# Gate halves stored in eight pieces, one per tile, and four down tiles that take the last gates from SBUF

## What is computed

```python
idx = e1 * N_KEYS + e2                       # N_KEYS = 128, so 128 x 128 experts
gates = jax.nn.softmax(sc, axis=-1)
u = peer_u[ix]
a = jax.nn.gelu(jnp.einsum('td,thkd->thk', hx, u), approximate=False)
vsel = peer_v[ix]
return jnp.einsum('thk,thkd->td', gx * a, vsel)
```

## Time and profile before

| | |
|---|---|
| median of 3 runs | 3111.55 us (3110.08 to 3111.72) |
| the profiled execution | 3113.11 us, span 3111.4 us |
| TensorE busy | 2941.4 us (95%) |
| VectorE, ScalarE, GpSimd busy | 1801.4, 1118.9, 1814.2 us |
| bytes moved | 539.11 MB, mean 173 GB/s |
| stores of gates | 12 of 2048 KB, median 16.3 us to landing |
| up stage | about 375 to 1090 us |
| down stage | about 1092 to 1600 us |

### The profile page before, as it was taken

The page is one execution under the profiler, slowest core; times in us unless marked ns, Lnnn a source line. Parts: engine busy times, 40 slices in busy tenths (PEclk is TensorE's granted clock), DMA queues, the critical chain, the costliest instruction groups (busy, mean ns, idle before and its releaser), DMA issues. The chain is left out here.

```text
span 3111.4 us, 42451 instructions
## 1 busy us (share of the span) xinstructions
PE 2941.4 (95%) x14433; PEld 2468.3 (79%) x14433; DVE 1801.4 (58%) x2994; ACT 1118.9 (36%) x2318; POOL 1814.2 (58%) x1154
## 2 busy tenths in 40 slices
PE   6989999998898889999999989999999999999998
PEld 5757899997898878888887667888778887788886
DVE  7764269977654377888874443322377887423225
ACT  2232215554455235444443423220145552322103
POOL 5525686676787745555543234666657664466664
PEclk9999999999999999999999999999999999999999
DMA  8412254566688989999972012223221111222332
GB/s 312 149 70 83 96 162 142 184 220 237 223 298 290 334 338 400 407 406 396 409 281 75 28 55 82 100 94 102 94 82 64 59 61 48 81 94 94 102 102 74
DMA packets 167757, 539.11 MB, mean 173 GB/s; under 512 B 15584, under 2 KB 73056, under 8 KB 151136
## 3 DMA queue, kind: packets, MB, share of 16 engines
q1 hardware_dynamic: 82544, 301.62, 27.9%
q0 software_dynamic: 18432, 134.23, 10.9%
q10 hardware_dynamic: 66672, 101.99, 9.0%
HBM read 485.35 MB, written 52.43 MB: 173 GB/s over the span
## 5 line engine op out<-in xcount | busy, mean ns | idle before, releaser
L2527 POOL TENSOR_SCALAR whi<-ring 128x1024 fp32r<-128x1024 f32 x384 | 426.0, 1109 | 989.6 <-issue 514.1
L2529 POOL TENSOR_TENSOR wlo<-ring,whi 128x1024 fp32r<-128x1024 f32 x384 | 972.1, 2532 | 32.1
L561 PE MATMUL ps<-norm_hi,whi 128*128 128x384 f32 (+1 forms) x1288 | 494.0, 384 | 20.6 <-ACT A L1413 11.9
L563 PE MATMUL ps<-norm_hi,wlo 128*128 128x384 f32 (+1 forms) x1288 | 454.5, 353 | 0.0
L562 PE MATMUL ps<-norm_lo,whi 128*128 128x384 f32 (+1 forms) x1288 | 453.1, 352 | 0.0
L561 PE MATMUL ps<-whi,mixed_hi 128*128 128x512 f32 x768 | 300.5, 391 | 11.5 <-DVE wlo L2123 8.7
L562 PE MATMUL ps<-wlo,mixed_hi 128*128 128x512 f32 x768 | 299.6, 390 | 0.0
L563 PE MATMUL ps<-whi,mixed_lo 128*128 128x512 f32 x768 | 299.5, 390 | 0.0
L2553 POOL TENSOR_TENSOR wlo<-ring,whi 128x512 fp32r<-128x512 f32 x126 | 166.2, 1319 | 228.5 <-ACT whi L1517 228.5
L561 PE MATMUL ps<-mix_hi,whi 128*128 128x512 f32 x744 | 290.6, 391 | 0.0
L563 PE MATMUL ps<-mix_hi,wlo 128*128 128x512 f32 x744 | 289.5, 389 | 0.0
(11 more groups left out here) (362 smaller groups left out, 6013.4 us busy)
## 6 DMA issues: line engine op xcount, KB each, us to landing
ring<-stream SPq DMA_DIRECT2D x519, 512.0 KB, 3.4
gelu_map<-A ACTq DMA_DIRECT2D x128, 192.0 KB, 2.9
gate_map<-A ACTq DMA_DIRECT2D x12, 2048.0 KB, 16.3
A<-gelu_map ACTq DMA_DIRECT2D x128, 192.0 KB, 10.8
A<-gate_map ACTq DMA_DIRECT2D x32, 768.0 KB, 13.0
A<-ada_w SPq DMA_DIRECT2D x10, 2048.0 KB, 8.1
A<-ada_w SPq DMA_DIRECT2D x4, 1024.0 KB, 22.7
X<-x_in SPq DMA_DIRECT2D x1, 2048.0 KB, 18.9
```

Source lines behind the costliest of these rows:

```text
L561: first = mm(out_, lh, rh, start=start, stop=False)
L563: return first, mm(out_, ll, rh, start=False, stop=stop)
L2527: g.tensor_scalar(h[:], raw[:], 1.0, 0.0, ALU.mult, ALU.add).then_inc(whi_ready, 1)
L2529: g.tensor_tensor(rest[:], raw[:], h[:].bitcast(F32), ALU.subtract).then_inc(split_ready, 1)
```

## The change

- A half is stored in eight pieces of 512 KB, one DMA each, instead of two of 2048 KB. A piece goes out at the end of ScalarE's work for each of the first eight tiles (b % 16 < 8) of the next half. The last half goes out in two pieces in each of the first four tail tiles.
- The counts: one semaphore for the first halves (eight pieces, 128 a phase), two for the second halves (four pieces, 64 a phase each). All waits on stores follow.
- In the tail, the eight loads of Gelu rows go out two a tile in tiles 0 to 3. The first load of gates goes out at k = 2 and takes five of six parts; the last 64 tokens' gates of the first four down tiles come from `staging[1]`, with a second, small product of VectorE. The load for the tiles from 4 on stays at k = 5.
- The high and low parts of the mixed rows change places (planes 36 to 39 and 32 to 35), and the first low part waits until all four mixes have read the staging plane.

```diff
+PIECES = 8
-PARTS_AT = dict(mixed=(32, 36), ...
+PARTS_AT = dict(mixed=(36, 32), ...
-            def store_gates(phase, half):
+            def store_gates(phase, half, e):
                 act.wait_ge(gate_bank_free, 2 + phase * AMONG + (half + 1) * AMONG // 2)
-                for q in range(2):
-                    g = slice(q * NKEY // 8, (q + 1) * NKEY // 8)
-                    r = slice(q * NKEY // 2, (q + 1) * NKEY // 2)
-                    act.dma_start(gate_map[g, :, 2 * phase + half, :].rearrange("g j n -> j g n"),
-                                  staging[half][:, r, :].rearrange("p (g i) t -> p g (i t)", i=4)).then_inc(gate_stored[q], 16)
+                g = slice(e * NKEY // 4 // PIECES, (e + 1) * NKEY // 4 // PIECES)
+                r = slice(e * NKEY // PIECES, (e + 1) * NKEY // PIECES)
+                act.dma_start(gate_map[g, :, 2 * phase + half, :].rearrange("g j n -> j g n"),
+                              staging[half][:, r, :].rearrange("p (g i) t -> p g (i t)", i=4)).then_inc(gate_stored[half and 1 + e // 4], 16)
                     if phase and b % 16 == 0:
-                        for q in range(2):
-                            act.wait_ge(gate_stored[q], 16 * (2 * phase - 1 + half))
+                        for part in ((0,), (1, 2))[half]:
+                            act.wait_ge(gate_stored[part], (128, 64)[half] * phase)
-                    if b % 16 == 15:
-                        store_gates(phase, half)
+                    if b % 16 < PIECES and (phase or half):
+                        store_gates(phase - 1 + half, 1 - half, b % 16)
-            def load_gates(m):
+            def load_gates(m, parts=2 * len(DENSE)):
-                act.dma_start(gate_ring[:, m // 4 % 2], gate_map[m // 4:m // 4 + 1].rearrange("g j b n -> (g j) b n"))\
+                act.dma_start(gate_ring[:, m // 4 % 2, 0:parts, :],
+                              gate_map[m // 4:m // 4 + 1, :, 0:parts, :].rearrange("g j b n -> (g j) b n"))\
-                if k == 1 or k == 3:
-                    for q in range(2):
-                        act.wait_ge(gate_stored[q], 16 * 5)
-                    for s in range(4):
-                        load_mixed(2 * (k - 1) + s)
+                if k < 4:
+                    for e in range(2 * k, 2 * k + 2):
+                        store_gates(len(DENSE) - 1, 1, e)
+                    act.wait_ge(gate_stored[0], 128 * len(DENSE))
+                    for s in range(2 * k, 2 * k + 2):
+                        load_mixed(s)
+                if k == 2:
+                    load_gates(0, 2 * len(DENSE) - 1)
                 if k == 5:
-                    for q in range(2):
-                        act.wait_ge(gate_stored[q], 16 * 6)
-                    for m in (0, 4):
-                        load_gates(m)
+                    for part in (1, 2):
+                        act.wait_ge(gate_stored[part], 64 * len(DENSE))
+                    load_gates(4)
+                if n >= 4:
+                    v.tensor_tensor(a, a, gate, ALU.mult).then_inc(mixed_ready, 1)
+                    return
+                dve.wait_ge(gate_bank_free, 2 + len(DENSE) * AMONG)
+                last = 2 * len(DENSE) - 1
+                v.tensor_tensor(a[:, 0:last, :], a[:, 0:last, :], gate[:, 0:last, :], ALU.mult)
+                v.tensor_tensor(a[:, last, :], a[:, last, :], staging[1][:, n, :], ALU.mult).then_inc(mixed_ready, 1)
+                if n == 0:
+                    dve.wait_ge(mixed_ready, 4)
             for n in range(4):
                 mix(n)
-                if n:
-                    low_mixed(n - 1)
+            for n in range(3):
+                low_mixed(n)
```

## The result

| | before | after |
|---|---|---|
| median | 3111.64 us (3110.08 to 3114.05, 4 runs) | 3088.03 us (3085.86 to 3088.54, 4 runs) |
| profiled execution, span | 3113.11, 3111.4 us | 3088.54, 3086.8 us |
| ratio of the times | | 0.9913, 95% interval 0.9899 to 0.9927 |

The change takes 23.6 us off by the medians, 24.6 us by the two profiled spans; the step sum had 26.5. The sum is close, but two of its terms were wrong in opposite directions. Where the time came from is read in three places. In all rows that follow, three points stand for rows left out.

The account below looks back on a forecast made before the run. TensorE, 95% busy, was taken to bound the kernel, stalled through ScalarE's held store issues. 28 us mid-phase plus 3 tail less 4.5 pressure gave 26.5 off 3113.11, so 3086.6, or 3085.0 at the median; range 3069 to 3103.

Parts of the forecast that it names:

- pairs 1 and 2: Gate stores at about 552 and 635 us: no long TensorE stall, 0 to 1 us lost, 0.5 us given back.
- pair 3: Gate stores at about 740 us: 12.9 us lost over four tiles, 9 given back (bounds 5 and 12.9).
- pair 4: Gate stores at about 847 us: 7.0 us lost over two plain and two one-hot tiles, 6.5 given back.
- pair 5: Gate stores at about 948 us: 13.3 us lost over four tiles, 12 given back.
- pressure of pieces in phase 2: Pieces in 16 tiles of phase 2 fill the DMA engines, up to 12 gathers late; 4.5 us lost (bounds 0 and 10).
- tail stretch: Last Gelu copies to first down product, DMA engines full: 3 us gained, bounds 0 and 13.
- Rival 2: Issues of pieces still block ScalarE, the tail loses 5 and late gathers cost 10: 13 us gained, 3098.5; chance 0.20.
- VectorE is next late: At the third pair, VectorE's own work nearly fills four tiles of 5.1 us, so only 9 of 12.9 us return.
- Rival 4: VectorE is late on its own at the third to fifth pairs; within 6 us of before; chance 0.05.
- the sum that begins with "17.5 MB": Tail: 17.5 MB less 1.2 already moved, at 0.392 MB per us, takes 41.6 us; first down product at 1091.7.
- Rival 1: TensorE rules the tail and phase 2 absorbs the pieces: 40 us gained, 3071.5; chance 0.18.
- The rule on batches: Skill advice to batch transfers to 1 MiB and more; a 512 KB piece costs up to 0.1 us more, 5 us DMA time.

Follow-up runs that it names:

- repeat: The changed kernel run and profiled once more with nothing changed; 3089.5 us, ratio 0.9922 to the kernel before.
- the tail in order of need: Changed kernel with tail Gelu stores on SyncE, first four mixed-row loads and first gates load ahead of the pieces, fifth mix behind first down tile; 3085.62 us, ratio 0.9912.

## Why the prediction was right, and where it was not

Forecast 3085.0 (3069 to 3103), measured 3088.03. By its own terms (spans; 24.6 us in all):

| term | forecast | measured |
|---|---|---|
| pairs 1 and 2, up to tile 69 | +0.5 | -2.4 |
| pair 3 (69-85) | +9 | +8.8 |
| pair 4 (85-89) | +6.5 | +4.9 |
| pair 5 (103-107) | +12 | +13.0 |
| pressure of pieces in phase 2 (89-103, 107-119) | -4.5 | -0.3 |
| tail stretch | +3 | -3.0, repeat -1.2 |
| down stage and the rest | 0 | +3.6 |

- **Held issues: right, and shown.** The chain from a held ScalarE over the share of an expert row to VectorE and TensorE was the cost of the middle. Pairs from SyncE, bursts and all, give back the same 8, 5 and 13 us at the places of pairs 3, 4 and 5. Rival 2 (the new issues are held too) is false in the middle and true in the tail. "VectorE is next late" at pair 3 held: 2.73 us of gap are left, for VectorE. Rival 4, little returns, fell with it.
- **Pairs 1 and 2: the bound was too narrow.** I had said 0 to 1 us. The time to tile 56 is 1.4 us longer with a new wait of 1.73 us for the split of a weight tile at 643.59, and 56-69 is 1.0 us longer with the same gap of TensorE (4.22 us, at 725.69 before and 726.28 after), but a granted clock of 0.72 instead of 0.86 over 724 to 736. That is 6.7 us at 1.2 GHz instead of 3.4. The pieces alone don't decide it: with the same middle and a gap of 4.21 us, the kernel with the tail in order of need had 3.4 us again and 77.80 us for 56-69. What does decide it stays open.
- **Pressure in phase 2: term over-sized.** I added up shares to 1.08 and charged 0.8 us for each of twelve gathers. The windows show 0.97 and 0.99, with one row late by 1.1 us among the pieces, and TensorE lost 0.3. The mistake is that a landing that is longer costs only once it passes its dot's need. In the trace before, only one gather in three has the tightest 7.6 us from issue to dot; the others have 10.4 or more. The term is real one step on: 1 MB a tile costs 15.0 us, 2 MB at once 9.6.
- **The tail: the step that failed.** It is the sum that begins with "17.5 MB". By it the last tile's Gelu copy comes at 1089.8, 46.5 us after tile 119's, which for 17.5 MB is 377 GB/s over the whole stretch. Measured are 50.2 us, 18.7 MB and 373 GB/s; in the repeat 48.4 us, 17.8 MB and 367 GB/s. So bytes that the sum lacked are worth 3.3 us (0.8 in the repeat), and the rate 0.5 (1.2). The bytes were missing in ScalarE's queue, which moved 8.6 MB (8.4) and not 7.6: the second load of gates, 0.79 MB at 1062.11, and one more Gelu store. The sum also took the last copy for one that waits for a store; in after it waits 3.67 us for TensorE, and the one before it 4.58, so the transfers ruled only the copies ahead of these. Another 2.0 us I put on top myself: the sum said 1.0 us sooner than before, and I took 3, for a last gather that would come late enough. The kind of bound was right: without the last half's stores the stretch falls by what the bytes are worth, and the ten kernels that keep nearly all of them (18.4 to 19.9 MB) take 48.0 to 54.2 us, whoever waits. Rival 1 (TensorE rules the tail, 3071.5) is out. Only a strict order of need got to 46.1, and only fewer bytes to 40.
- **Two errors cancel.** The pressure was 4.2 us too dear and the tail 4 to 6 us too cheap, and 3.6 us came from parts that the change doesn't touch. The total was right to 3.0 us, a good deal better than the working was; that is luck. The rule on batches, which spoke against small pieces, did not show: the Trainium skill (DMA: Bandwidth & Descriptors, section "Bandwidth") asks for 1 MiB and more in a transfer, and here 1024 KB cost 15.0 us and 2048 KB, eight tiles apart, 9.6 us in phase 2 over the 512 KB pieces. Nobody waits for a piece, so its own fixed cost is hidden, and what a large one takes from gathers and Gelu stores isn't.
- **Down start and down stage.** The extra product and wait were hidden as said: the down start gap is 2.25 us, was 2.68. The 3.6 us that the rest of the run gives differ from kernel to kernel where nothing was changed (down stage 532.5 to 536.7 us without moved gathers), so I give them no cause. Behind the down stage, where nothing was changed either, the profiles differ by up to 10 us (1480 to 1490), so the total of a single run says less than its stretches.

## What to carry to other kernels

Look at the duration of DMA issues on an engine that also computes: a transfer that nobody waits for can still stop the engine that issues it, and the cost shows two engines further on. Cutting it into pieces near the size that the DMA engines have free per step, and spreading them, took most of that back here: 26.7 of the 33.2 us that I had counted at pairs 3 to 5. Where the engines are already full, only fewer bytes or a strict order of need shortened the stretch, and a held issue there is a symptom. When a forecast adds up bytes over a rate, count the bytes per queue over the real stretch in the trace, and take the rate from a mix of transfers like the new one.

## What was not expected of the hardware

- The hold follows the queue, not the DMA engines. With the pairs on SyncE, that engine was held 8.37 us at 937.37 and 8.62 at 1032.08, while none of ScalarE's 128 Gelu stores took over 0.36 us to issue. How much a queue takes before it holds was not settled. By an estimate from before and after, the bytes issued on ScalarE's queue less those moved, it had some 1.4 to 2.9 MB ahead at the start of a hold.
- Three kinds of traffic together (gathers, 512 KB weight tiles, stores and loads of small runs) moved 362 to 385 GB/s at a share of 0.98 to 1.03 over the tail stretch, depending on order, queue and size. The prediction had used 392 for it, read over a window 4 us shorter.
- The same gap of 4.2 us was followed by 3.4 us at the lower clock in two kernels (before, and the tail in order of need) and by 6.7 us in the changed one, whose middle is that of the second.
